# One model's attention steps put directly behind each other, and the other's compressed scores in one bank with turn copies on one engine

## The reference

```python
def first_block(x, ...):
    for l in range(DEPTH):
        x = x + 0.5 * swiglu(rms_norm(x, ffn1_norm[l]), ...)
        x = x + hybrid_mixer(rms_norm(x, mix_norm[l]), ...)
        x = x + 0.5 * swiglu(rms_norm(x, ffn2_norm[l]), ...)
    return rms_norm(x, final_norm)

def second_block(x, ...):
    for l in range(DEPTH):
        x = hybrid_layer(x, ...)          # x + mixed @ w_out
    return rms_norm_2(x, final_g)
```

```python
s = jnp.einsum('bqghd,bngd->bghqn', qb, k_cmp) * scale
p_cmp = masked_softmax(s, cmp_end[None, :] <= tq[:, None])
o_cmp = jnp.einsum('bghqn,bngd->bqghd', p_cmp.astype(dt), v_cmp)
o = gb[..., 0:1] * o_cmp + gb[..., 1:2] * o_slc + gb[..., 2:3] * o_win
```

## Time and profile before

| | us |
|---|---|
| three runs, median | 1661.79 |
| three runs, lowest and highest | 1661.53, 1663.7 |
| the profiled execution's own time | 1663.86 |
| its span | 1662.1 |
| PE busy | 1620.4 (97%) |
| DVE busy | 948.8 (57%) |
| ACT busy | 797.2 (48%) |

### The profile page before, as it was taken

One profiled execution on the slowest core, in us unless ns is written; L12 is line 12 of the kernel. 1 busy time (PEld: TensorE's weight loads), 2 busy tenths in 40 slices (PEclk: granted clock), 3 DMA queues, 4 the chain that ended last, 5 costly groups with the idle time before them and its releaser, 6 DMA issues.

```text
span 1662.1 us, 23070 instructions
## 1 busy us (share of the span) xinstructions
PE 1620.4 (97%) x8818; PEld 1370.7 (82%) x8818; DVE 948.8 (57%) x1449; ACT 797.2 (48%) x1340; POOL 157.8 (9%) x183
## 2 busy tenths in 40 slices
PE   7999999999999999999999999999999999999997
PEld 6888899878888887888899977888888879777885
DVE  5555564444665545555466444655554878567874
ACT  6444465444364445444365444354444455453542
POOL 0000012111200000000012211210000201000100
PEclk9999999999999999999999999999999999999998
DMA  7666455434455554655546443455665552254421
GB/s 247 200 207 206 152 183 174 135 127 133 146 186 184 188 189 159 200 187 183 184 147 200 134 137 111 153 176 192 202 209 171 168 177 83 68 181 147 142 69 51
DMA packets 76430, 269.61 MB, mean 162 GB/s; under 512 B 8480, under 2 KB 9504, under 8 KB 76320
## 3 DMA queue, kind: packets, MB, share of 16 engines
q1 hardware_dynamic: 76320, 268.14, 49.0%
HBM read 267.06 MB, written 1.05 MB: 161 GB/s over the span
## 4 chain that ended last, share of the span: by engine, by line
PE 90%; DVE 5%; ACT 2%; issue 1%; DMA 1%; POOL 1%; DVEq 0%; POOLq 0%; SPq 0%; ACTq 0%
PE bank L337 26%; PE bank L339 25%; PE bank L338 25%; PE bank L342 8%; PE bank L347 5%; DVE wlo L289 1%; ACT hh L353 1%; DVE hl L373 1%; ACT wk L362 1%; DVE cv L373 1%; DMA raw<-W 1%; POOL stat L365 0%; DVE x L373 0%; ACT whi L283 0%; DVE nmt L1565 0%
## 5 line engine op out<-in xcount | busy, mean ns | idle before, releaser
L289 DVE TENSOR_TENSOR wlo<-raw,whi 128x1024 fp32r<-128x1024 f32 (+4 forms) x468 | 560.3, 1203 | 404.4 <-ACT whi L283 382.7
L283 ACT ACTIVATE whi<-raw 128x1024 fp32r<-128x1024 f32 (+3 forms) x496 | 509.2, 1034 | 443.8 <-PE bank L339 419.3
L337 PE MATMUL bank<-whi,hh 128*128 128x512 f32 (+4 forms) x1312 | 497.5, 379 | 6.6 <-DVE hl L373 3.7
L339 PE MATMUL bank<-whi,hl 128*128 128x512 f32 (+4 forms) x1312 | 486.2, 371 | 0.0
L338 PE MATMUL bank<-wlo,hh 128*128 128x512 f32 (+4 forms) x1312 | 485.3, 370 | 0.0
L337 PEld LDWEIGHTS bank<-whi,hh 128*128 128x128 f32 x1312 | 247.7, 189 | 51.1 <-DVE hl L373 7.0
L339 PEld LDWEIGHTS bank<-whi,hl 128*128 128x128 f32 x1312 | 247.3, 188 | 40.1
L338 PEld LDWEIGHTS bank<-wlo,hh 128*128 128x128 f32 x1312 | 247.8, 189 | 35.7
L337 PE MATMUL bank<-hh,whi 128*128 128x256 f32 x480 | 143.7, 299 | 0.0
L339 PE MATMUL bank<-whi,gl 128*128 128x512 f32 x352 | 138.7, 394 | 0.0
L338 PE MATMUL bank<-wlo,gh 128*128 128x512 f32 x352 | 137.9, 392 | 0.0
(11 more groups left out here) (293 smaller groups left out, 1710.2 us busy)
## 6 DMA issues: line engine op xcount, KB each, us to landing
raw<-W SPq DMA_DIRECT2D x464, 512.0 KB, 3.3
raw<-W SPq DMA_DIRECT2D x26, 384.0 KB, 3.6
raw<-W SPq DMA_DIRECT2D x8, 416.0 KB, 2.9
tab<-tab SPq DMA_DIRECT2D x6, 384.0 KB, 4.0
raw<-W SPq DMA_DIRECT2D x4, 426.0 KB, 3.4
raw<-W SPq DMA_DIRECT2D x6, 192.0 KB, 2.8
x<-x_in SPq DMA_DIRECT2D x2, 512.0 KB, 5.8
tab<-gains SPq DMA_DIRECT2D x2, 512.0 KB, 4.3
```

What stands on the lines that cost most here:

```text
L283: high = act.op(lambda e: e.activation(whi[i][:, 0:w], r[:, 0:w], ACT.Copy), self.landed[c], free)
L289: tok = (low or dve).op(lambda e: e.tensor_tensor(wlo[i][:, 0:w], r[:, 0:w], whi[i][:, 0:w].bitcast(F), ALU.subtract), self.landed[c], hig ...
L337: pe.op(lambda e: e.matmul(dst, ah, bh, start=start, stop=False), *tokens, mark=False)
L339: return pe.op(lambda e: e.matmul(dst, al, bh, start=False, stop=stop), mark=mark)
```

## The change

In the first mixer, an iteration of `Att.run` issues T, V, the finishing steps that are due, and S in one go, and yields the number of them as its weight. moba with dil is 23 such iterations of the total weight 78 in the gates' 48 steps, and dil's steps count double, as was written before but not passed on by `limited`. In the second mixer, the compressed scores of both halves go into one bank, and the softmax steps follow earlier; all turn copies go to ACT.

```diff
@@ -772,17 +772,19 @@
                 n = len(units)
                 for i in range(n + self.lag + 1):
                     due, self.later2, self.later = self.later2, self.later, []
+                    steps = 0
+                    if 0 <= i - self.lag < n:
+                        self.turn(units[i - self.lag])
+                        steps += 1
+                    if 0 <= i - self.lag - 1 < n:
+                        self.values(units[i - self.lag - 1])
+                        steps += 1
+                    for f in due:
+                        f()
                     if i < n:
                         self.scores(units[i])
-                        yield
-                    if 0 <= i - self.lag < n:
-                        self.turn(units[i - self.lag])
-                        yield
-                    for f in due:
-                        f()
-                    if 0 <= i - self.lag - 1 < n:
-                        self.values(units[i - self.lag - 1])
-                        yield
+                        steps += 1
+                    yield steps
                 for f in self.later2 + self.later:
                     f()
 
@@ -1056,8 +1058,8 @@
                             return gate_tok[t, n]
                         yield from row_group("branch_gate", 8, 2, 512, H, norm.ready, take, ring=MM, fine=True)
 
-                heads = iter_chain(attend("moba", make_units, 256), (2 for _ in attend("dil", make_units, 768)))
-                weave(limited(heads, 55), 74, gate_tiles(), 48)
+                heads = iter_chain(attend("moba", make_units, 256), (2 * n for n in attend("dil", make_units, 768)))
+                weave(limited(heads, 23), 78, gate_tiles(), 48)
                 h_free = h_last()
 
 
@@ -1120,10 +1122,9 @@
                             turn_merged(0)
                         yield
                 both = branches()
-                for steps in (1, 2, 2):
+                for _ in range(2):
                     next(both)
-                    for _ in range(steps):
-                        next(heads)
+                    next(heads)
                 next(both)
                 drain(heads)
                 yield from both
@@ -1141,9 +1142,10 @@
 
         def limited(gen, n):
             for _ in range(n):
-                if next(gen, "end") == "end":
+                got = next(gen, "end")
+                if got == "end":
                     return
-                yield
+                yield got
 
         nm_at = [0]
 
@@ -1572,7 +1574,7 @@
                 u["group"]["last"]["exp"] = u["exp"]
                 ring.give(i, u["exp"])
 
-            turned_n, late = [0], [False]
+            late = [False]
 
             def turn(u):
                 m = 2 * (u["t"] + 1)
@@ -1582,9 +1584,7 @@
                 for k in range(m):
                     tok = tr(bank[:, k * 128:(k + 1) * 128], u["buf"][:, k * 128:(k + 1) * 128], u["exp"], free,
                              mark=(k == m - 1))
-                turned_n[0] += 1
-                f = v_copy if turned_n[0] % 3 == 0 else a_copy
-                u["got"] = f(pt[:, 0:m * 128], bank[:, 0:m * 128], tok, pfree)
+                u["got"] = a_copy(pt[:, 0:m * 128], bank[:, 0:m * 128], tok, pfree)
                 TT.give(i, u["got"])
                 sring.give(u["i"], tok)
 
@@ -1668,18 +1668,20 @@
                 s0 = [cw[:, t, 0:120] for t in range(2)]
                 s3 = [z.rearrange("p (h n) -> p h n", n=15) for z in s0]
                 d1, d3, e1, d7, d8 = [], [], [], [], []
+                i, bank, free = XB.take()
                 for t in range(2):
-                    cm = kc[:, K_CM + t * 15:K_CM + (t + 1) * 15].unsqueeze(1).broadcast_to([128, 4, 15])
-                    i, bank, free = XB.take()
                     for h in range(4):
                         q2, k2 = ([z[:, h, t * 128:(t + 1) * 128] for z in (qTh, qTl)],
                                   [z[:, :, :].rearrange("p g n -> p (g n)") for z in (kch, kcl)])
-                        tok = mm3(bank[:, h * 32:(h + 1) * 32], q2, k2, True, True, kct, free, mark=(h == 3))
+                        tok = mm3(bank[:, t * 128 + h * 32:t * 128 + (h + 1) * 32], q2, k2, True, True, kct, free,
+                                  mark=(t == 1 and h == 3))
+                for t in range(2):
+                    cm = kc[:, K_CM + t * 15:K_CM + (t + 1) * 15].unsqueeze(1).broadcast_to([128, 4, 15])
                     d1.append([stt(s3[t][:, 4 * g:4 * g + 4, :],
-                                   bank[:, 0:128].rearrange("p (h g n) -> p g h n", h=4, g=2)[:, g, :, 0:15],
+                                   bank[:, t * 128:(t + 1) * 128].rearrange("p (h g n) -> p g h n", h=4, g=2)[:, g, :, 0:15],
                                    -1.0, cm, ALU.mult, ALU.add, tok, base) for g in range(2)])
-                    XB.give(i, d1[t][1])
-                    yield from pause(3)
+                XB.give(i, d1[1][1])
+                yield from pause(2)
                 for t in range(2):
                     mx = sm[:, 224 + t * 24:224 + t * 24 + 8]
                     d2 = dve.op(lambda e, mx=mx, z=s3[t]: e.tensor_reduce(mx, z, AX, ALU.max), d1[t])
```

## The result

| | us |
|---|---|
| before, 4 runs: median, lowest to highest | 1661.84, 1661.53 to 1663.7 |
| after, 4 runs: median, lowest to highest | 1651.74, 1650.78 to 1653.54 |
| ratio, 95% interval | 0.9938, 0.9921 to 0.9955 |
| the profiled execution of after: its own time, its span | 1650.99, 1649.2 |

Forecast were 1649.0, with 1643.5 to 1657 as the range.

The account below looks back on a forecast made before the run. TensorE (PE), busy 97% of the span, was taken to bound the kernel. Terms −0.9 (first mixer), −1.3 (copies), −5.9 (tail), −4.4 (clock) sum to −12.5 us: 1649 from the 1661.79 median, range 1643.5 to 1657.

Parts of the forecast that it names:

- First mixer: First mixer with steps grouped: one wait goes, less a grouping loss; net −0.9 us, ends −1.9 and +1.0.
- The wait on bl: First mixer's last branch block: PE's 0.93 us wait in each layer goes, 1.9 us saved.
- The loss by grouping: First mixer: scores no longer stand directly ahead of a turn, at most 1.0 us lost.
- The wait on the exponential: First mixer's last attention part: 5.2 us between scores and turn cover the 3.5 us needed; costed at nothing.
- Turn copies: Second mixer, all turn copies on ACT: shorter waits where DVE is busy, −1.3 us, ends 0 and −5.8.
- Tail: Second mixer's tail: oc's gating directly behind ysl, qTh 2.95 us earlier in each layer; −5.9 us, ends 0 and −7.9.
- The wait for oc: Second mixer's tail: PE waits about 2 us for oc's transposes, in place of waits of 2.20 and 1.50.
- Clock: Three low-clock stretches lose 6.7 us, 2.3 of it kept after the change; −4.4 us, ends 0 and −6.7.
- rival 1: The clock falls as before, at other places: gain 8.1 us, 1653.7 us; chance 0.20.
- Rival 3: All four places of the tail fall to 1.2 GHz: gain 5.9 us, 1655.9 us; chance 0.08.
- Rival 4: First mixer's turn waits for the exponential, at 1 us a unit +16: slower, 1665 us; chance 0.04.
- Rivals 2 and 5: Tail's gain moves elsewhere, 1657 us, chance 0.15; changed order moves waits that end nothing, 1661.8 us, chance 0.05.

Follow-up runs that it names:

- the late kernel: The changed kernel, both halves still in one bank but the softmax three steps later (pause 5 instead of 2): 1665.97 us, ratio 1.002.
- the fill with transposes: The changed kernel with 17 transposes of a constant put into the 2.0 us wait ahead of oc's transposes in each layer: 1649.72 us.
- the fill with matmuls: The changed kernel with 16 matmuls of 256 columns on constants in the 2.0 us wait ahead of oc's transposes in each layer: 1651.72 us.

## Why the prediction was right, and by how much each step was off

The time lay in the range and 2.7 us above the point. Step by step, in the profiled pair:

- **First mixer, forecast −0.9, measured −1.5.** The wait on bl went as said. The loss by grouping was put at 1.0 us (11 × 0.04 × 2 is 0.9), and next to none of it is seen. The wait on the exponential was put at nothing and is 0.18 us in each layer: the gap of 5.2 us was worked out for the 768 wide units, and dil's first unit, whose iteration has only its scores in it, has 2.7 (353.57 to 356.27). What the prediction did not see is why the grouping is needed: aT early but ungrouped brings a wait of 0.57. And it put the shared bank of the last scores down to the compressed scores, while the first mixer's part causes it.
- **Turn copies, forecast −1.3, measured 0.** The waits in the busy stretch shrank, from 1.50 to 0.56 at the place named, but in the profile of the first mixer's part alone, with the copies as before, that wait had already come down to 1.08 by itself. The stretches ahead of the tails are 1.3 us shorter in the changed kernel, but already 0.33 and 0.31 us shorter in that one, where no edit touches them; with the 0.13 and 0.34 of the copies that is 1.1 of the 1.3. What the copies gave there they take back in the tails, 0.3 to 0.4 us in each, where the last turn waits for a copy on ACT. The step costed DVE's queue and not ACT's at the other end of the layer.
- **Tail, forecast −5.9, measured −7.0.** The mechanism is the one described: the compressed scores alone bring it, and the late kernel takes it away. The wait for oc was forecast at about 2 and was 2.00. The first output block starts when it did, as forecast: 9.99 us after the last weight block ahead of the tail (1421.20 to 1431.19), before 10.03 (1423.25 to 1433.28). That the order by itself brings it forward by 0.9 us, and that the shared bank and the copies on ACT take as much back, was not foreseen. The term is too small behind that: the way from the conv product to qTh, 13.99 us in the earlier trace rows, was forecast at 11.0 and is 1451.88 − 1439.93 = 11.95, of which the low clock took 1.46, so 10.5 by itself. The transposes and the ysh matmuls had been entered as 0.66 + 5.86 = 6.52 us, with ends that overlap what follows; at full clock they take 6.07.
- **Clock, forecast −4.4, measured −3.1 in the profiled pair** (6.0 lost before, 2.9 after, by the starts). The 6.7 that the forecast began with were too much, since its window at 1638 has idle time in it. At most one low stretch was to remain and two did, one in each layer: rival 1, the falls at other places, came half true. Rival 3, by the Trainium skill ("TensorE: Matmul & The Clock Gate", section "Part 4: PE-mode transpose"), by which transposes don't count as busy in the way that matmuls do, fell: two of the four places of the tail did, not all. Nor did the low stretches simply stay with 17 transposes in place of the idle time, as they would by that sentence of the Trainium skill: three of these four runs have a mean clock of 0.998 to 0.999. That speaks against the sentence for this kernel's fp32 transposes, but the one profile of that kernel fell earlier, so it isn't settled.
- **Sum.** −12.5 was forecast for the profiled pair and −12.9 measured (1663.86 to 1650.99): the errors of the terms cancel, which is luck. Between the medians it is 10.1: the profiled run of before lay 2.1 us above its median, that of after 0.75 below, and the prediction took the same offset for both.
- **Rivals 2, 4 and 5.** Rival 4's wait is there only at dil's first unit, with 0.18 us and not 1 us a unit. At the wide units no turn waits for its exponential: the scores at 376.48 have their turn at 382.18, 5.7 us later (forecast 5.2). Rivals 2 and 5 would have kept the waits of 2.20 and 1.50 or their like, and none stands behind oc.

## What to carry to other kernels

When an engine's queue is a fixed order, look for the short chain that starts late and stands in front of everything else: moving its first step up by three places was worth 9 us here, order and clock together, while evening out the load of two engines (the copies) was worth nothing. A wait that goes should be followed one chain further: the wait for oc that was left was in the forecast with its number, and covering it with a block of weights that was there anyway (and gating oc a step earlier) gave another 6 us.

Two edits of one change can meet in shared state, as the banks' order did here; run each alone before a wait is put down to one of them.

## What was not expected of the hardware

The granted clock doesn't fall at the same places in every kernel with the same order of work: behind the compressed scores, with PE busy all the time, it fell in the fill with transposes (0.58 at 1409 to 1413) and not in the fill with matmuls (1.00). A wait of 2.0 us ahead of oc's transposes was followed by 0.57 in the changed kernel and by 1.00 in the kernel with the compressed scores alone, whose clock had fallen behind these scores (0.60 at 1412 to 1416). In the 51 runs of the kernel before, times and mean clock vary together over 4.8 us (1661.2 to 1666.0), more than three of the four terms of the sum.
